# Expert down-projection pieces loaded with rows 2p and 2p+1 in partition p, and the activation transposed from every other column

## The chip, the core and the metric

The kernel runs on one core of one Trainium2 chip. The metric is device microseconds of that core, from the start of the program to its end. The kernel before takes 1797.82 us (median of 3 runs, 1796.47 to 1798.79).

## The reference

One encoder block over 512 tokens of width 1024: a norm, a wide input projection, a gated linear recurrence in both directions and a windowed attention, both merged and projected back, and then a mixture of 32 experts with the top 4 for each token. The change is in the experts:

```python
def expert_block(args):
    xblk, e = args
    hu = xblk @ w_up_gate[e] + b_up_gate[e]          # 1024 -> 2048
    g, u = hu[:, :D_FF_EXPERT], hu[:, D_FF_EXPERT:]
    g = jnp.minimum(g, SWIGLU_LIMIT)
    u = jnp.clip(u, -SWIGLU_LIMIT, SWIGLU_LIMIT)
    act = g * jax.nn.sigmoid(SWIGLU_ALPHA * g) * (u + 1.0)
    return act @ w_down[e] + b_down[e]               # 1024 -> 1024
```

`w_down[e]` is 1024 x 1024 in fp32, 4 MB; `w_up_gate[e]` is 1024 x 2048, 8 MB. The product `act @ w_down[e]` is a sum over 1024 rows of `w_down`, each with its own column of `act`. In which order and in which groups of 128 the rows are taken is free, as long as rows and columns go together.

## The kernel before

Each expert handles one block of up to 96 tokens (`BLK = 96`). All weights stream through SBUF once, in pieces of 1 MB: 128 partitions of 2048 fp32 values. An expert has 12 pieces, 8 of the up matrix (128 rows of 8 KB each, one row in a partition) and 4 of the down matrix (256 rows of 4 KB, two rows in a partition). A piece passes three stages. The SP queue loads it into one of 6 raw slots (`load_piece`, line 504, DMA at line 510), ACT copies it to fp32r as its high part `wH` (line 421), and DVE subtracts to get the low part `wL` (line 1687), each with 4 slots. SP waits before a load until DVE is done with the slot's former piece (`wait_split`, line 412). PE then multiplies three times for each pair of operands, high x high, high x low and low x high (`mm3`, lines 321 to 323).

The PE loop over experts (lines 1016 to 1020) does, for expert i: the up product of i, with the transposes of expert i-1's activation in it after its second piece (`a_part`, line 983), the transposes of the next expert's gathered tokens (`x_part`, line 936), and the down product of i-1 (`down_part`, line 995). The order of all engines is written out by hand.

`a_part` turns the activation `actv` (96 tokens x 1024) into eight tiles of 128 x 96. Each is one weight load of 96 x 128 from `actv` and one matmul with a 96 x 96 identity. Tile k becomes `aTH[:, k, :]` and `aTL[:, k, :]`. `down_part` multiplies tile `2 * q + kk` with half `kk` of piece q in its slot:

```python
def half_piece(kk, n):
    return slice(kk * D + n * 512, kk * D + (n + 1) * 512)
...
for kk in range(2):
    for n in range(2):
        last = mm3(bank[yb + n][0:BLK, :], high_[:, 2 * q + kk, :], low_[:, 2 * q + kk, :],
                   wH[:, slot, half_piece(kk, n)], wL[:, slot, half_piece(kk, n)], ...)
```

Of the kernel before, what the change touches and what calls it, by code (L numbers as in the profile page):

```python
# [35 lines left out]
P = 128  # L36
# [11 lines left out]
BLK = 96  # L48
# [55 lines left out]
def build(nc, x, norm_mix_gain, w_in, hg_lb_fwd, hg_lb_bwd, hg_norm_gain, attn_sink, w_out,  # L104
# [201 lines left out]
    bank = [nc_psum[:, i * 512:(i + 1) * 512] for i in range(8)]  # L306
# [7 lines left out]
    ident = cst[:, K_ID:K_TF]  # L314
# [94 lines left out]
    def first(i):  # L409
        return isinstance(i, int) and i == 0  # L410
# [52 lines left out]
    with nc.Block() as block:  # L463
# [3 lines left out]
        def _(sp):  # L467
# [45 lines left out]
                return w_up_gate[0][bass.ds(e, 1), p * P:(p + 1) * P, :].rearrange("o p n -> (o p) n")  # L513

            def down_src(e, q):
                return w_down[0][bass.ds(e, 1), q * 2 * P:(q + 1) * 2 * P, :].rearrange("o (k p) n -> p (o k) n", p=P)

            sp.wait_ge(w_lo, PRE_B + 8 * NH)
            for q in range(2):
# [28 lines left out]
            def load_body(e):  # L548
                for p in range(8):
                    load_piece(e, p, up_src(e, p))  # L550
                for q in range(4):
                    load_piece(e, 8 + q, down_src(e - 1, q))
# [12 lines left out]
            for q in range(4):  # L565
                load_piece(NE, q, down_src(NE - 1, q))
# [16 lines left out]
            def overflow(i, code):  # L583
                e = nc.s_assert_within(code >> NBC_BITS, 0, NE - 1, skip_runtime_bounds_check_because="codes are below NE * NBC")
                sp.wait_ge(x_ready, NT)
                for p in range(8):
                    load_piece(i, 4 + p, up_src(e, p))
                for q in range(4):
                    load_piece(i + 1, q, down_src(e, q))
# [12 lines left out]
        def _(pe):  # L602
# [5 lines left out]
            for k in range(KD):  # L608
                for j in range(NT):
                    if k == 0:  # L610
                        pe.wait_ge(xn0, j + 1)
                    last = nc.tensor.transpose(bank[k][:, j * P:(j + 1) * P], xt[:, j, k * P:(k + 1) * P], ident)
# [330 lines left out]
            def up_part(i, over=False, turn_last=False):  # L943
# [15 lines left out]
                for p in range(8):  # L959
                    if first(i):  # L960
                        pe.wait_ge(xTl_ready, p + 1)
                    wait_split(pe, k, b0 + p)
                    slot = (b0 + p) % SPLIT
                    for n in range(4):
                        cols = slice(n * 512, (n + 1) * 512)
                        last = mm3(bank[n][0:BLK, :], xTH[:, p, :], xTL[:, p, :], wH[:, slot, cols], wL[:, slot, cols], False, p == 7)
                    last.then_inc(p_used, 1)
                    if first(i) and p == 3:
                        table()
                    if turn_last and p == 1:  # L970
                        a_part(i - 1, 2 * i + KD)
                    if isinstance(i, int) and i == NE - 1 and p == 4:
                        turn_gates()
# [9 lines left out]
            def a_part(i, x_before):  # L983
                pe.wait_ge(act_ready, i + 1)
                pe.wait_ge(xTl_ready, x_before)
                if not first(i):
                    pe.wait_ge(aTl_ready, 2 * i)
                if isinstance(i, int) and i == NE - 1:
                    pe.wait_ge(gt_step, 3)
                for b_ in range(2):  # L990
                    for k in range(4 * b_, 4 * b_ + 4):
                        last = nc.tensor.transpose(bank[6 + b_][:, (k % 4) * BLK:(k % 4 + 1) * BLK], actv[0:BLK, k * P:(k + 1) * P], ident[0:BLK, 0:BLK])  # L992
                    last.then_inc(aT_done, 1)

            def down_part(i, over=False, turn_next=False, high_=aTH, low_=aTL):
                k, b0 = down_at(i, over)
                yb = Y_BANK[i] if isinstance(i, int) and i in LATE else 4
                if isinstance(i, int) and i == LATE[1]:
                    pe.wait_ge(sg_ready, NE)
                elif not first(i) and not over:  # L1000
                    pe.wait_ge(y_ready, i)
                pe.wait_ge(aTl_ready, 2 * i + 2)
                for q in range(4):
                    wait_split(pe, k, b0 + q)
                    slot = (b0 + q) % SPLIT
                    for kk in range(2):
                        for n in range(2):
                            last = mm3(bank[yb + n][0:BLK, :], high_[:, 2 * q + kk, :], low_[:, 2 * q + kk, :], wH[:, slot, half_piece(kk, n)],
                                       wL[:, slot, half_piece(kk, n)], 2 * q + kk == 0, 2 * q + kk == KD - 1)
                    last.then_inc(p_used, 1)  # L1010
                    if turn_next and q == 1:
                        a_part(i + 1, 2 * NE - 2 + KD)
# [58 lines left out]
            def overflow(i):  # L1071
                pe.wait_ge(aTl_ready, 2 * i)
                pe.wait_ge(x_ready, NT * (i - (NE - 1)))
                x_part(i)
                up_part(i, True)
                a_part(i, 2 * i + KD)
                down_part(i, True)
                pe.wait_ge(place_set, 4 * (i - LATE[0]) + (4 + TOPK))
                pe.wait_ge(yL_ready, i - LATE[0] + 1)
                for j in range(NT):  # L1080
                    combine(0, j, True, True)
# [1105 lines left out]
```

## Time and profile before

| | before |
|---|---|
| median of 3 runs | 1797.82 us |
| the profiled execution's own time | 1797.82 us |
| its span | 1796.1 us |
| PE busy | 1756.1 us (98%) |
| DVE busy | 1426.3 us (79%) |
| ACT busy | 1143.2 us (64%) |
| mean DMA rate over the span | 272 GB/s |
| one high part (ACT, line 421) / one low part (DVE, line 1687) | 1919 / 2288 ns |

Times are microseconds in one profiled execution, counted from the start of the span. PE is TensorE's matmul side and PEld its weight loads, which overlap with the matmuls. SPq is the queue of SyncE, which issues nearly all DMAs. A line number names the line of the kernel that made the instruction; where a helper makes it, as `mm3` does, the operands tell the use. In the chain of waits each piece is listed with the time for which nothing else held up the end, so eight transposes count there from the first start to the next instruction's start.

### The profile page before, as it was taken

How to read it: one execution, taken by the hardware profiler on the slowest of the kernel's cores; microseconds unless marked ns; L12 is line 12 of the kernel's file. 1: busy time of each engine (PE TensorE's matmuls, PEld its weight loads, DVE VectorE, ACT ScalarE, POOL GpSimd, SP SyncE). 2: the span in 40 equal slices, each digit the busy share in tenths (PEclk: the TensorE clock that was granted, in tenths of full speed). 3: DMA queues.
4: the chain of work that ended last, by engine and by line, in shares of the span. 5: the costliest groups of instructions: out<-in, count | busy, mean ns of one | idle time of the engine just before them, and what ended most of it. 6: DMA issues, size and time to landing. Idle time of an engine off the chain costs nothing.

```text
span 1796.1 us, 26530 instructions
## 1 busy us (share of the span) xinstructions
PE 1756.1 (98%) x8973; PEld 1286.9 (72%) x8973; DVE 1426.3 (79%) x1461; ACT 1143.2 (64%) x1122; POOL 316.3 (18%) x244
## 2 busy tenths in 40 slices
PE   6999999999999989999999999999999999999997
PEld 5777777777778856777777777777777777777765
DVE  4565665576557688988898889889888988898898
ACT  4534554454454556777777777777777777777783
POOL 0012102201210111211211121112111211211153
PEclk9999999999999989999999999999999999999999
DMA  7431332233116469999999999999999999999995
GB/s 207 130 87 55 105 93 73 67 105 104 36 61 224 178 244 342 402 382 380 365 368 367 379 365 369 370 365 380 359 376 371 366 369 378 366 370 367 376 341 235
DMA packets 159058, 488.44 MB, mean 272 GB/s; under 512 B 13186, under 2 KB 83122, under 8 KB 125520
## 3 DMA queue, kind: packets, MB, share of 16 engines
q1 hardware_dynamic: 151936, 471.48, 71.9%
q0 software_dynamic: 7088, 16.52, 2.7%
q8 instruction: 20, 0.33, 0.1%
q14 instruction: 14, 0.11, 0.0%
HBM read 479.43 MB, written 24.39 MB: 281 GB/s over the span
## 4 chain that ended last, share of the span: by engine, by line
PE 93%; DVE 3%; DMA 2%; issue 1%; SPq 1%; ACT 0%; POOL 0%; DVEq 0%; POOLq 0%; ACTq 0%
PE psum L321 27%; PE psum L323 26%; PE psum L322 26%; PE psum L956 1%; PE psum L690 1%; PE psum L720 1%; PE psum L706 1%; PE psum L940 1%; PE psum L992 1%; PE psum L673 1%; DVE wL L1687 1%; DMA wraw<-in_w_down 1%; PE psum L657 1%; PE psum L667 1%; PE psum L747 1%
## 5 line engine op out<-in xcount | busy, mean ns | idle before, releaser
L1687 DVE TENSOR_TENSOR wL<-wraw,wH 128x2048 fp32r<-128x2048 f32 x388 | 882.2, 2288 | 122.5 <-ACT wH L421 119.8
L421 ACT ACTIVATE wH<-wraw 128x2048 fp32r<-128x2048 f32 x388 | 743.9, 1919 | 296.2 <-PE psum L323 279.7
L321 PE MATMUL psum<-wH,xTH 128*96 128x512 f32 x1040 | 417.3, 401 | 2.9 <-DVE wL L1687 2.8
L323 PE MATMUL psum<-wH,xTL 128*96 128x512 f32 x1040 | 409.1, 393 | 0.0
L322 PE MATMUL psum<-wL,xTH 128*96 128x512 f32 x1040 | 408.9, 393 | 0.0
L321 PEld LDWEIGHTS psum<-wH,xTH 128*96 128x96 f32 x1040 | 168.4, 162 | 76.0 <-DVE wL L1687 2.8
L323 PEld LDWEIGHTS psum<-wH,xTL 128*96 128x96 f32 x1040 | 168.2, 162 | 72.7 <-issue 0.2
L322 PEld LDWEIGHTS psum<-wL,xTH 128*96 128x96 f32 x1040 | 168.4, 162 | 69.5
L321 PE MATMUL psum<-wH,aTH 128*96 128x512 f32 x496 | 197.1, 397 | 0.3 <-DVE wL L1687 0.3
L323 PE MATMUL psum<-wH,aTL 128*96 128x512 f32 x496 | 194.6, 392 | 0.0
L322 PE MATMUL psum<-wL,aTH 128*96 128x512 f32 x496 | 194.2, 391 | 0.0
L2095 POOL COPY ixg<-tab 128x2 int32 (+1 forms) x31 | 22.8, 734 | 557.6 <-PE psum L940 543.9
L321 PE MATMUL psum<-tsH,xnH 128*128 128x512 f32 (+1 forms) x288 | 112.2, 390 | 0.0
L321 PE MATMUL psum<-xnH,wsH 128*128 128x512 f32 x272 | 109.7, 403 | 0.1
L323 PE MATMUL psum<-tsH,xnL 128*128 128x512 f32 (+1 forms) x288 | 109.0, 379 | 0.0
L322 PE MATMUL psum<-tsL,xnH 128*128 128x512 f32 (+1 forms) x288 | 109.0, 378 | 0.0
L323 PE MATMUL psum<-xnH,wsL 128*128 128x512 f32 x272 | 106.2, 391 | 0.0
L322 PE MATMUL psum<-xnL,wsH 128*128 128x512 f32 x272 | 106.0, 390 | 0.0
L2099 POOL DMA_INDIRECT xg<-x2d,ixg x31 | 101.5, 3273 | 24.1 <-POOL ixg L2095 24.1
L323 PEld LDWEIGHTS psum<-wH,aTL 128*96 128x96 f32 x496 | 80.0, 161 | 35.0
L322 PEld LDWEIGHTS psum<-wL,aTH 128*96 128x96 f32 x496 | 80.2, 162 | 32.3
L321 PEld LDWEIGHTS psum<-wH,aTH 128*96 128x96 f32 x496 | 79.9, 161 | 32.7 <-DVE wL L1687 0.8
(272 smaller groups left out, 2178.3 us busy)
## 6 DMA issues: line engine op xcount, KB each, us to landing
wraw<-in_w_up_gate SPq DMA_DIRECT2D x256, 1024.0 KB, 6.9
wraw<-in_w_down SPq DMA_DIRECT2D x128, 1024.0 KB, 7.7
fraw<-in_w_in SPq DMA_DIRECT2D x68, 512.0 KB, 4.1
yd<-in_consts SPq DMA_DIRECT2D x8, 1024.0 KB, 8.4
wraw<-yd SPq DMA_DIRECT2D x3, 2048.0 KB, 11.0
wraw<-in_w_out SPq DMA_DIRECT2D x4, 1024.0 KB, 6.0
xt<-in_x SPq DMA_DIRECT2D x4, 512.0 KB, 6.5
hres<-in_x SPq DMA_DIRECT2D x4, 512.0 KB, 5.3
```

The costliest lines, as they stand in the source:

```text
L321: nc.tensor.matmul(ps, lh, rh, start=start, stop=False)
L322: nc.tensor.matmul(ps, lh, rl, start=False, stop=False)
L323: return nc.tensor.matmul(ps, ll, rh, start=False, stop=stop)
L421: nc.scalar.activation(wH[:, b % SPLIT, :], raw(b), ACT.Copy).then_inc(p_hi, 1)
L657: last = nc.tensor.matmul(bank[4 + 2 * d + c][:, j * P:(j + 1) * P], kt[rows_of, j, :], vv[rows_of, j, :], start=True, stop=True)
L667: nc.tensor.matmul(ps, ss[:, j, :], vv[:, j, :], start=True, stop=False, skip_group_check=True)
L673: last = nc.tensor.matmul(half, qd[:, tok], S[:, n, :], start=False, stop=True, skip_group_check=True)
L690: nc.tensor.matmul(bank[4 + a][:, 0:len(tiles) * P], aqT[half, n * P:(n + 1) * P], kcur[half, tiles[0] * P:(tiles[-1] + 1) * P], start=Tru ...
L706: last = nc.tensor.transpose(bank[2 + a][:, i * P:(i + 1) * P], sbuf_p[:, a, i * P:(i + 1) * P], ident)
L1687: V.tensor_tensor(wL[:, b % SPLIT, :], raw(b), wH[:, b % SPLIT, :].bitcast(F32), ALU.subtract).then_inc(p_lo, 1)
L2095: G.tensor_copy(ixg[:, :], src).then_inc(ix_ready, 1)
L2099: gp.indirect_dma_start(xg[0:BLK, :], None, x2d, bass.IndirectOffsetOnAxis(ap=ixg[0:BLK, 0:1], axis=0), bounds_check=last_token, oob_is_er ...
```

## The change

In the load of the down matrix (`down_src`), partition p of piece q held rows 256q + p and 256q + 128 + p, two runs of 4 KB. It now holds rows 256q + 2p and 256q + 2p + 1, which are neighbours in memory: one run of 8 KB, and the whole piece is one contiguous megabyte. Half kk of the slot thus holds the rows 256q + 2p + kk. The transposes follow: tile k, which was columns 128k to 128k + 127 of `actv`, is now the 128 columns 256 (k // 2) + k % 2 + 2p. Everything behind them is as it was.

```diff
             def down_src(e, q):
-                return w_down[0][bass.ds(e, 1), q * 2 * P:(q + 1) * 2 * P, :].rearrange("o (k p) n -> p (o k) n", p=P)
+                return w_down[0][bass.ds(e, 1), q * 2 * P:(q + 1) * 2 * P, :].rearrange("o (p k) n -> p (o k n)", k=2)
...
                     for k in range(4 * b_, 4 * b_ + 4):
-                        last = nc.tensor.transpose(bank[6 + b_][:, (k % 4) * BLK:(k % 4 + 1) * BLK], actv[0:BLK, k * P:(k + 1) * P], ident[0:BLK, 0:BLK])
+                        last = nc.tensor.transpose(bank[6 + b_][:, (k % 4) * BLK:(k % 4 + 1) * BLK], actv[0:BLK, (k // 2) * 2 * P + k % 2:(k // 2 + 1) * 2 * P:2], ident[0:BLK, 0:BLK])
```

No instruction is added, removed or moved on any engine. On SP the loads of the down matrix alone have another shape. This is expert 0's place, straight ahead of the loop over the other experts:

```order
 L540 DMA x2d<-xr 128x1024
 L510 DMA wraw<-in_w_up_gate 128x2048 x8
-L510 DMA wraw<-in_w_down 128x2x1024 x4
+L510 DMA wraw<-in_w_down 128x2048 x4
 L559 DMA over_list<-ovi 128x1
 L560 DMA gate_of<-gates 128x4x4
```

The four loads stand where they stood; what was 2 x 1024 values for each partition is one run of 2048, the shape of the up matrix's loads above them.

## Rows read from the trace of the kernel before

**Rows 1.** The page, part 1: busy time of each engine, share of the span.

```profile
PE 1756.1 (98%) x8973; PEld 1286.9 (72%) x8973; DVE 1426.3 (79%) x1461; ACT 1143.2 (64%) x1122; POOL 316.3 (18%) x244
```

**Rows 2.** Busy time by stretch; columns as the header row says.

```profile
core 0: us, PE busy (x) PEld busy (x) DVE busy (x) ACT busy (x) POOL busy (x), PEclk, DMA share, GB/s
657.94:693.30 35.36, 33.55 (x154) 22.90 (x152) 31.28 (x31) 20.89 (x15) 2.46 (x2) 1.00 0.89 257
693.40:1744.80 1051.40, 1051.40 (x4865) 741.93 (x4866) 933.79 (x564) 783.21 (x539) 201.28 (x125) 1.00 0.98 373
1744.80:1796.10 51.30, 39.38 (x160) 26.10 (x158) 44.89 (x37) 20.48 (x24) 20.47 (x8) 0.91 0.60 236
```

**Rows 3.** Chain of waits, one expert's period: start us, us, what.

```profile
1018.26 0.66 PE psum L992 x8
1035.54 0.66 PE psum L940 x8
...
1053.70 0.66 PE psum L992 x8
```

**Rows 4.** Waits, 700 to 1711 us: engine line waited for, us, times, longest.

```profile
ACT wH L421 <- PE psum L323: 253.1, 303, 0.9
...
ACT wH L421 <- DMA wraw<-in_w_up_gate: 4.2, 5, 1.7
ACT wH L421 <- DMA wraw<-in_w_down: 3.5, 4, 1.7
```

**Rows 5.** DMA issues of the page: count, KB each, us to landing.

```profile
wraw<-in_w_up_gate SPq DMA_DIRECT2D x256, 1024.0 KB, 6.9
wraw<-in_w_down SPq DMA_DIRECT2D x128, 1024.0 KB, 7.7
```

**Rows 6.** Waits of the SP queue, 700 to 1711 us.

```profile
SPq L510 <- DVE wL L1687: 803.6, 344, 3.7
```

**Rows 7.** Line 510's own issues on SP: ns min/median/max, first and last.

```profile
L510 SPq DMA_DIRECT2D wraw<-in_w_up_gate x256: 327/333/943, 565.3 to 1720.5; - x128
...
L510 SPq DMA_DIRECT2D wraw<-in_w_down x128: 367/376/384, 657.9 to 1744.9; - x128
```

**Rows 8.** Timeline of SP, first loads of the second matrix: start us, us.

```profile
657.94 12.50 SPq L510 DMA_DIRECT2D wraw<-in_w_down  x4
...
671.00 0.52 SPq L560 DMA_DIRECT2D gate_of<-gates  x1
```

**Rows 9.** Busy time by stretch around the first such loads.

```profile
676.00:679.00 3.00, 3.00 (x15) 2.10 (x14) 3.00 (x2) 2.16 (x2) 0.00 (x0) 1.00 2.25 106
679.00:682.00 3.00, 3.00 (x20) 2.28 (x19) 3.00 (x3) 0.05 (x1) 1.45 (x1) 1.00 0.05 22
```

**Rows 10.** Chain of waits, the last of expert 0's four such loads.

```profile
670.07 14.73 DMA wraw<-in_w_down
```

**Rows 11.** Timeline of ACT and PE: what stood still behind the late load.

```profile
684.82 1.91 ACT L421 ACTIVATE wH<-wraw 128x2048 fp32r<-128x2048 f32 x1 [5.77 <-DMA wraw<-in_w_down]
...
693.38 0.48 PE L321 MATMUL psum<-wH,xTH 128*96 128x512 f32 x1 [0.38 <-DVE wL L1687]
```

**Rows 12.** Waits of ACT on the pieces, 1711 to 1796 us.

```profile
ACT wH L421 <- PE psum L323: 10.1, 11, 2.3
...
DVE wL L1687 <- ACT wH L421: 4.1, 8, 1.3
```

**Rows 13.** Weight loads by line and shape: count, busy us, mean ns.

```profile
L322 PEld LDWEIGHTS psum<-wL,xTH 128*96 128x96 f32 x1040 | 168.4, 162 | 69.5
...
L322 PEld LDWEIGHTS psum<-tsL,xnH 128*128 128x128 f32 x288 | 54.3, 188 | 9.2
...
L992 PEld LDWEIGHTS psum<-cst,actv 96*128 96x128 f32 x256 | 24.8, 140 | 6.8 <-DVE actv L1896 1.9
...
L980 PEld LDWEIGHTS psum<-cst,gd 128*96 128x96 f32 x4 | 0.5, 126 | 0.2
```

**Rows 14.** Timeline of PE, one expert's eight transposes of the activation.

```profile
699.13 0.82 PE L992 MATMUL psum<-cst,actv 96*128 96x96 f32 x8
```

## Prediction

> **What bounds the kernel now.** I read the page's busy shares first, then busy time by stretch, then the chain of waits over one expert, and last what waits for DMA. TensorE is busy for 98% of the span [rows 1]. By stretch the picture is sharper [rows 2]: from 693.40 to 1744.80 us, which is the experts' loop, it is busy 1051.40 of 1051.40 us at a granted clock of 1.00. There is no idle time there to give back, whatever the transfers do. The chain over one expert consists of PE pieces alone, and the activation's eight transposes stand in it with 0.66 us at 1018.26, as the eight transposes of the gathered tokens do at 1035.54 [rows 3]. So the time of an expert is a sum of PE work, and the reader should look for two things only: whether the change alters PE work, and whether anything in the few stretches where PE idles hangs on the second matrix's loads.
>
> In the same window ACT, the first user of every piece, waited 3.5 us in 4 waits for the second matrix and 4.2 us in 5 waits for the first, of 1011 us; its 303 other waits were for PE to free a buffer [rows 4]. None of it reached PE.
>
> **The change, part by part.**
>
> *The loads.* 128 pieces of 1 MB each arrive in partition runs of 8 KB instead of two of 4 KB. Their shape is then that of the first matrix's pieces: same bytes, same 128 partitions, one run each. The page prices both: 7.7 us median to landing for the second matrix, 6.9 for the first [rows 5]. I take 6.9 for the new form, 0.8 less. The two medians are taken at different places of the queue, so 0.8 is an estimate; between 0 and twice that changes nothing below. In the loop a piece that lands 0.8 us sooner lies ready longer: the SP queue spent 803.6 us of 1011 waiting for DVE to free a slot [rows 6], so the loads run as fast as slots come free and not the reverse. Worth on the path: 0. What would be late next if that cover were gone: ACT's split, 7.7 us of waits in all [rows 4], and behind it DVE and PE.
>
> *Their issue.* One issue of such a load costs SP 376 ns, one of the first matrix's 333 [rows 7]; 4 x 43 ns an expert, in a queue that waits for most of the loop. Worth 0. The order and the waits of all five engines stay as they are.
>
> *The one place where a late load shows.* Expert 0's four loads of the second matrix are issued from 657.94 on, and a small write of gates follows them at 671.00 [rows 8]. Between 676 and 682 us the queues move 106 and then 22 GB/s [rows 9], and the last of the four lands 14.73 us after its release [rows 10]. ACT stands for 5.77 us before that piece, and 8.6 us later PE loses 0.38 us to DVE's low part [rows 11]. A faster load can give back that 0.38 us. The bound is all idle time of PE between the first such load and the steady loop, 35.36 - 33.55 = 1.81 us [rows 2]; the other bound is 0, since the hole at 676 to 682 us is no matter of run length (the first matrix's loads stand in it as well) and may lie as before or a little later. I take 0.3 us gained, near the 0.38 that the row shows. Before 657.94 no load of the second matrix exists, so that part can't change.
>
> *The end.* After 1744.80 PE idles 51.30 - 39.38 = 11.92 us [rows 2]. ACT's eleven waits for pieces there are all for PE, none for a DMA [rows 12]. Worth 0.
>
> *The transposes.* This is the only part on the path. Their number stays 8 x 32 = 256, with the activation as the weight load (96 x 128) and the identity streaming. What changes is that the load reads every other 4-byte column, 8 bytes apart, where it read neighbours. No row of before shows a weight load with such a step, so I bound it. How much room is there? Loads in transposes take 140 ns for 128 columns and 126 for 96 [rows 13]: (140 - 126) / 32 = 0.44 ns a column, so 56 ns of the 140 are reading, the rest a latency. Plain fp32 loads take 188 and 162: 0.81 ns a column, 104 ns for 128. Eight transposes take 0.82 us from the first start to the last end [rows 14] and 0.66 / 8 = 82.5 ns each on the chain [rows 3]. A read of 56 ns hides under 82.5 ns with 26 to spare.
> Lower bound: 0, a step can't make the read cheaper than neighbours, and the pace is not set by the load. Upper bound, if the step halves the rate: the read takes 104 (the plain fp32 rate) to 112 ns (twice 56), that is 22 to 30 ns over the pace, times 256 is 5.6 to 7.7 us, all of it exposed because PE has no idle time. Between these the room decides: the step may slow the read by up to 82.5 / 56 = 1.47 times at no cost. I take 0, since the rows give nothing that ties the rate to distance.
>
> The Trainium skill has a rule against this part: "SBUF — State Buffer", Door 1 (the note on cachelines), says that SBUF is read in lines of 16 bytes and that two accesses to a line are needed for the full rate, with a penalty where each access goes to a new line. No row here shows a stepped read, so the trace neither confirms nor denies it. With an 8-byte step two columns share a line, so by this rule the transposes stay free; by the same rule a step of 16 bytes would be the costly one. Its "DMA: Bandwidth & Descriptors", section Bandwidth (why small descriptors are slow), puts a fixed overhead on each descriptor; by it the loads gain a little from halving their number, and rows 5 agree in sign.
>
> **The sum.** The profiled execution took 1797.82 us, span 1796.1, which is also the median of the three runs (1796.47 to 1798.79). 1797.8 - 0.3 (start of the loop) + 0 (loads in the loop) + 0 (issue) + 0 (transposes) = 1797.5 us.
>
> **The rivals.**
> 1. *The transposes' weight load halves its rate* (slower). Place: line 992, each of the 256. It decides from 1.47 times the present read. For it: fp32 loads at 0.81 ns a column exist in this trace, so the path can run at that pace, and PE has no slack. Against it: the loads in transposes run at 0.44, and 26 ns are free. Time: 1797.5 + 5.6 to 7.7 = 1803.1 to 1805.2, middle 1804.
> 2. *Each stepped column costs a whole read of its own* (slower, rarer): four times the read, 224 - 82.5 = 141 ns, times 256 = 36 us, 1834. Only a step that defeats the read path entirely would do that; nothing in the rows speaks for it.
> 3. *The faster loads matter more than the rows say* (faster): expert 0's piece lands early, the loop starts 1.8 us sooner and nothing replaces it. Time: 1796.0. To get beyond 3.6 us something in a fully busy PE stretch would have to speed up with the shape of a transfer; matmuls of this loop would then have to start closer together. I see no row for it.
> 4. *The change doesn't do what it says*: the queue could cut a run of 8 KB into two pieces again, and the landing stays 7.7 us. The first matrix's 6.9 speaks against it. Time 1797.8, the same answer on the clock.
>
> **How the numbers follow.** What a measurement of this kernel can tell from no change is 0.2%, 3.6 us: 1794.2 to 1801.4. The forecast with rival 4 has 0.66, rival 3 within the bound 0.07, rival 3 beyond it (or an unknown gain) 0.05, rival 1 0.18, rival 2 with other unknown losses 0.04. So faster 0.05, same 0.73, slower 0.22. The range goes from 1795.0 (rival 3's 1796.0 less the runs' own 1 us) to 1804.5, which takes in most of rival 1.
>
> **What would show each step right or wrong.** The chain's entry for the eight transposes: 0.66 us if the step is free, 0.83 to 0.9 by rival 1; the mean of their weight load at 140 ns, or near 190. The transposes of the gathered tokens are the control: they must stay at 0.66. The period between two experts is 1053.70 - 1018.26 = 35.44 us [rows 3] if I am right, and 0.18 to 0.24 more by rival 1. The second matrix's landing should be about 6.9 us and its issue about 333 ns. ACT's 5.77 us wait should shrink and PE still be busy without a gap from about 693 to 1744 us. A PE idle total in the loop that is not zero, or matmuls of the loop at another pace, would make the forecast wrong in a way that none of the cases holds.

## The result and the profile after

The changed kernel takes 1805.93 us (median of 5 runs, 1804.88 to 1807.3) against 1796.47 us for the kernel before in its company (5 runs, 1795.38 to 1798.79). The ratio is 1.0049, 95% interval 1.0037 to 1.0061: 8.8 us slower (6.6 to 11). Forecast were 1797.5 us and no change, with 1804.5 as the upper end of the range. The profiled execution took 1806.29 us, its span is 1804.5.

First the chain of waits of the changed kernel over one expert (start us, us, what), which answers to [rows 3]:

```profile
697.87 0.92 PE psum L992 x8
715.41 0.66 PE psum L940 x8
...
733.58 0.92 PE psum L992 x8
```

The eight transposes of the activation (line 992) count 0.92 us where they counted 0.66. Those of the gathered tokens (line 940), which the change doesn't touch, still count 0.66. From one expert to the next it is 733.58 - 697.87 = 35.71 us, where it was 35.44. That is 0.27 us an expert and 32 x 0.27 = 8.6 us in all.

The weight loads of both kinds of transposes, by line and shape (count | busy us, mean ns | idle before), against [rows 13]:

```profile
L992 PEld LDWEIGHTS psum<-cst,actv 96*128 96x128 f32 x256 | 35.5, 211 | 5.2 <-DVE actv L1896 1.8
L940 PEld LDWEIGHTS psum<-cst,xg 96*128 96x128 f32 x248 | 24.4, 143 | 9.7 <-DMA xg<-x2d,ixg 4.8
```

211 ns in place of 140 for line 992; line 940 stays at the 143 ns it had before. And busy time by stretch (columns as in [rows 2]):

```profile
657.94:693.30 35.36, 34.70 (x159) 24.09 (x158) 32.02 (x30) 21.49 (x15) 2.49 (x2) 1.00 0.89 266
693.40:1744.80 1051.40, 1051.40 (x4832) 745.97 (x4831) 926.37 (x560) 777.13 (x534) 199.96 (x122) 1.00 0.97 370
```

PE is still busy without a gap in the loop, but in the same stretch it gets through fewer instructions: 4832 in place of 4865, and 33 matmuls of 0.23 us are 7.6 us. Nothing waits; PE itself has more to do.

The loads took the shape that the change asks for. The hardware queue's packets (count, MB, share of 16 engines) before, then after:

```profile
q1 hardware_dynamic: 151936, 471.48, 71.9%
q1 hardware_dynamic: 135552, 471.48, 71.3%
```

That is 16384 packets fewer for the same bytes, or 128 for each of the 128 pieces: one for each partition of a piece. A run of 8 KB is not cut in two again, and rival 4 of the prediction falls. The landing and the issues on SP:

```profile
wraw<-in_w_down SPq DMA_DIRECT2D x128, 1024.0 KB, 7.2
```

```profile
L510 SPq DMA_DIRECT2D wraw<-in_w_down x128: 327/333/339, 657.6 to 1751.7; - x128
```

The issue went from 376 to 333 ns [rows 7], and it does so in every run with 8 KB runs. The median landing went from 7.7 to 7.2 us [rows 5]. Over all profiled executions of this case it is 7.2 to 7.5 us in the five kernels with 8 KB runs and 7.3 to 8.0 us in the nine with 4 KB runs: lower by some 0.4 us, though the two spreads touch.

Behind expert 0's last load of the second matrix, ACT waited 4.85 us where it had waited 5.77 [rows 11], and PE's idle time between 657.94 and 693.3 us fell from 1.81 to 35.36 - 34.70 = 0.66 us. This can't be put down to the loads. In the kernels whose loads are those of before, that wait of ACT is anywhere from 2.75 to 5.77 us and the same idle time of PE from 0.83 to 1.81 us; in those with 8 KB runs it is 2.82 to 4.85 us and 0.66 to 2.19 us.

### The profile page after: what moved, and what is told of

Read it like the earlier page. It is cut to its first block, busy times and chain, and to the rows that moved or that the text cites. A ratio compares the mean times of both kernels' runs of the same rounds, so it can differ in the third digit from the quotient of the medians.

```text
span 1804.5 us, 26530 instructions
## 1 busy us (share of the span) xinstructions
PE 1766.1 (98%) x8973; PEld 1298.8 (72%) x8973; DVE 1426.2 (79%) x1461; ACT 1143.3 (63%) x1122; POOL 317.9 (18%) x244
## 4 chain that ended last, share of the span: by engine, by line
PE 95%; DVE 3%; DMA 1%; issue 1%; ACT 0%; SPq 0%; POOL 0%; DVEq 0%; POOLq 0%; ACTq 0%
PE psum L321 27%; PE psum L323 27%; PE psum L322 27%; PE psum L992 2%; PE psum L956 1%; PE psum L690 1%; PE psum L720 1%; PE psum L706 1%; PE psum L940 1%; PE psum L673 1%; DVE wL L1687 1%; PE psum L657 1%; PE psum L667 1%; DMA xg<-x2d,ixg 1%; PE psum L747 1%
```

## The experiments

Each kernel was run beside the kernel before on the same chip; a ratio is to that one, with its 95% interval. Short diffs are to the kernel before unless another is named.

### Loads alone

```diff
-  .rearrange("o (k p) n -> p (o k) n", p=P)
+  .rearrange("o (p k) n -> p (o k n)", k=2)
```

> The loads in 8 KB runs, the transposes as before (rows and columns no longer go together; the instructions and sizes are those of before). Theory A (all of the loss is in the stepped weight load of the transposes): the eight transposes count 0.66 us in the chain again, their weight load 140 ns, and the time is that of the kernel before, 0 to 1 us less (PE idled 1.15 us less between 657.94 and 693.3 us after the change). Theory B (the contiguous loads cost something, by the transfers' arrival or by contention): a part of the 9 us stays, and it would show as PE idle or matmuls further apart than 0.23 us.

1797.52 us against 1797.72, ratio 1.0002 (0.9993 to 1.0011). Its chain:

```profile
733.57 0.66 PE psum L992 x8
...
769.01 0.66 PE psum L992 x8
```

The period is 35.44 us again. The loads cost nothing and, within 0.1%, bring nothing. Theory B falls.

### Transposes alone

```diff
-  actv[0:BLK, k * P:(k + 1) * P]
+  actv[0:BLK, (k // 2) * 2 * P + k % 2:(k // 2 + 1) * 2 * P:2]
```

> The loads as before, the transposes from every other column (rows and columns no longer go together). Theory A: the whole loss, 8 to 9.5 us slower than before: 0.26 us in each of 32 groups of eight transposes, which count 0.92 us in the chain, with a weight load of about 211 ns. Theory B: less than 8 us, the rest belongs to the loads.

1804.6 us against 1797.72, ratio 1.0042 (1.0028 to 1.0056).

```profile
733.38 0.92 PE psum L992 x8
...
769.10 0.92 PE psum L992 x8
```

0.92 us and a period of 769.10 - 733.38 = 35.72 us: the loss of the changed kernel, from this line alone. Theory A holds. The loads of this kernel are those of before, and yet PE idles only 1.05 us between 657.94 and 693.3 us: the shorter idle time there comes without the 8 KB runs too.

### The cost doubled

```diff
 (against the changed kernel, line 940)
-  xg[0:BLK, k * P:(k + 1) * P]
+  xg[0:BLK, (k // 2) * 2 * P + k % 2:(k // 2 + 1) * 2 * P:2]
```

> The changed kernel, with the transposes of the gathered tokens stepping by two as well, which leaves their rows unmatched to the weights. The suspected cost is doubled: theory A says another 31 groups of eight at 0.26 us, 8 us more than the changed kernel, 16 to 18 us over the kernel before, the period of an expert at 35.98 us. If the loss is bound to the activation's place (its writer, its buffer), it is less.

1814.42 us against 1796.66, ratio 1.0096 (1.0081 to 1.0112): 17 us over the kernel before, twice the loss. The period of an expert is 35.97 us.

```profile
L992 PEld LDWEIGHTS psum<-cst,actv 96*128 96x128 f32 x256 | 35.5, 211 | 5.0 <-DVE actv L1896 1.9
L940 PEld LDWEIGHTS psum<-cst,xg 96*128 96x128 f32 x248 | 34.6, 212 | 8.4 <-DMA xg<-x2d,ixg 5.2
```

The tokens' loads now take 212 ns like the activation's. The buffer and its writer have no part in it (the tokens are written by a DMA, the activation by DVE).

### How the cost depends on the step

```diff
-  actv[0:BLK, k * P:(k + 1) * P]
+  actv[0:BLK, (k // 4) * 4 * P + k % 4:(k // 4 + 1) * 4 * P:4]   (4 apart)
+  actv[0:BLK, k:8 * P:8]                                         (8 apart)
+  actv[0:BLK, k * 126 + 1:k * 126 + 129]                         (neighbours, odd start)
```

> The loads as before; each transpose reads its 128 columns 4 apart (16 bytes), which leaves the order of rows and columns unmatched. Theory P (neighbouring fp32 columns are fetched in pairs, any step above 1 loses that): same as step 2, weight load 211 ns, eight transposes 0.92 us, 8 to 9.5 us slower than before. Theory L (the fetch is limited by the 16-byte lines it touches: a quarter line a column at step 1, half at step 2, one at step 4): from step 2 the read of about 132 ns doubles to 264, the weight load takes about 345 ns, a group of eight transposes about 2 us, and the kernel is some 42 us slower than before.

> The loads as before, the transposes' columns 8 apart (32 bytes); rows and columns unmatched. By the pair theory the same as steps 2 and 4: weight load about 214 ns, eight transposes 0.92 us. If distance counts at all, it is more here.

> The loads as before, the transposes read 128 neighbouring columns that begin at an odd column (126k + 1), so that no pair of columns is aligned to 8 bytes as before; the activation is not covered whole. If fp32 columns are fetched in aligned pairs of 8 bytes, this costs next to nothing (65 fetches in place of 64): 140 ns, 0.66 us. If the fast read needs an aligned start, it shows as the step does: 211 ns, 0.92 us.

The weight loads of line 992 with the columns 4 apart, 8 apart, and side by side from an odd start:

```profile
L992 PEld LDWEIGHTS psum<-cst,actv 96*128 96x128 f32 x256 | 35.7, 214 | 5.0 <-DVE actv L1896 1.9
```

```profile
L992 PEld LDWEIGHTS psum<-cst,actv 96*128 96x128 f32 x256 | 33.3, 203 | 5.4 <-DVE actv L1896 1.9
```

```profile
L992 PEld LDWEIGHTS psum<-cst,actv 96*128 96x128 f32 x256 | 24.9, 139 | 6.8 <-DVE actv L1896 1.9
```

214 ns at a step of 4, 203 at 8, against 211 at 2. The kernel with step 4 takes 1805.09 us against 1797.72, ratio 1.0040 (1.0025 to 1.0056); the other two are single runs (1802.77 and 1794.86 us, against 1796.66). The chain at step 8:

```profile
733.51 0.86 PE psum L992 x8
...
769.16 0.86 PE psum L992 x8
```

A greater distance costs next to nothing more (3 ns at step 4): theory L, with 345 ns and 42 us, is refuted. The load of neighbours from an odd column takes 139 ns. So what is lost is adjacency, and it is lost with the first step; alignment to 8 bytes isn't needed. One thing was not expected: at step 8 the group counts 0.86 us and not 0.92, and the period is 35.65 us, 0.21 over the kernel before and not 0.27. Every period of that trace shows it, and no run says why. That the fast read takes two neighbouring values at a time fits the rest, but it doesn't explain this, and the runs show rates, not the fetch itself.

### By the column or by the load?

Half the activation is left out here: seven of eight transposes take 64 columns. The first diff is side by side, the second with a step of two.

```diff
-  bank[6 + b_][:, ...], actv[0:BLK, k * P:(k + 1) * P]
+  bank[6 + b_][0:64 if k else P, ...], actv[0:BLK, k * P:k * P + (64 if k else P)]
+  bank[6 + b_][0:64 if k else P, ...], actv[0:BLK, k * P:k * P + (128 if k else 2 * P):2]
```

> The loads as before; seven of the eight transposes of a group take 64 neighbouring columns in place of 128, the first takes 128 (half of the activation is left out). The read at 0.44 ns a column: 112 ns for a weight load of 64 columns, 28 less than for 128. The pace of transposes stays at 82 ns, since the streaming identity sets it.

> The same with a step of two. If the step costs by the column, as two single reads in place of one pair (0.88 to 1.03 ns a column against 0.44), a weight load of 64 columns takes 140 to 150 ns and the read of 56 to 66 ns hides under the 82 ns of the identity: eight transposes count 0.66 to 0.7 us and the loss is gone. If the step costs a fixed time for each weight load, the load takes 112 + 74 = 186 ns and the group stays near 0.92 us.

Side by side, then with the step:

```profile
L992 PEld LDWEIGHTS psum<-cst,actv 96*64 96x64 f32 x224 | 19.4, 111 | 2.7
...
L992 PEld LDWEIGHTS psum<-cst,actv 96*128 96x128 f32 x32 | 4.5, 141 | 4.0 <-DVE actv L1896 1.9
```

```profile
L992 PEld LDWEIGHTS psum<-cst,actv 96*64 96x64 f32 x224 | 20.3, 138 | 1.0
...
L992 PEld LDWEIGHTS psum<-cst,actv 96*128 96x128 f32 x32 | 6.4, 200 | 4.0 <-DVE actv L1896 1.9
```

Side by side it is 111 ns for 64 columns and 141 for 128: (141 - 111) / 64 = 0.47 ns a column. With the step it is 138 for 64 and 200 for 128: (200 - 138) / 64 = 0.97 ns a column. With the shortest load of the changed kernel, 194 ns, it is (194 - 138) / 64 = 0.88. So a column takes about twice the time of before, 112 to 124 ns for 128 columns, and 64 stepped columns (138 ns) take what 128 neighbours take (140 ns). Both kernels were run once, 1798.91 us side by side and 1797.74 with the step, against 1796.36; the loss is read from the chain, here with 64 stepped columns:

```profile
734.32 0.66 PE psum L992 x8
...
769.77 0.66 PE psum L992 x8
```

0.66 us and a period of 35.45: a stepped read of 64 columns, 56 to 62 ns, hides under the 82.5 ns of the streaming identity, and the loss is gone. The cost goes by the column, and only what stands out over the matmul is paid.

### The step hidden under matmuls

```diff
 (against the changed kernel, in the third piece of the up product; the eight in a row after the second piece go)
+  for n in range(4):
+      matmul(bank[n], xTH, wH)
+      turn_one(2 * n)
+      matmul(bank[n], xTH, wL)
+      turn_one(2 * n + 1)
+      matmul(bank[n], xTL, wH)
```

> The changed kernel, with the eight transposes of the loop no longer back to back: each stands between two matmuls of the up product's third piece (same operands, same results, two of every three gaps taken). Theory A (the stepped weight load costs only where it is longer than what runs in front of it): the read of the transpose now lies under a matmul of 230 ns, each transpose adds 82 to 90 ns again, the period of an expert goes from 35.71 us back to 35.44 to 35.5, and the kernel is within 0.2% of the one before. Theory D (the stepped load holds the array or the fetch for itself and is not hidden): each transpose still adds 115 ns, period 35.71, 8 to 9.5 us slower than before. The transposed activation is complete some 2 us later, which ACT and DVE could turn into a wait of PE at line 956 or 1002; neither theory expects it, as they stand idle for 4 us or more an expert.

> Control for the spread transposes: the same placement between matmuls, but loads and transposes as in the kernel before (two runs of 4 KB, neighbouring columns). If the 0.09 us an expert that the spread kernel kept over the one before (period 35.53 us against 35.44) come from the change of neighbours between transposes and matmuls, they stay here: period 35.53 us, about 3 us over the kernel before. If they are what the hidden step still costs, the period is 35.44 and the time that of before.

With the step: 1799.98 us against 1796.66, ratio 1.0019 (1.0010 to 1.0028). The control with neighbouring columns: 1798.84 against 1797.35, ratio 1.0008 (0.9999 to 1.0017). The chain of the stepped one, where the transposes are line 994:

```profile
768.16 0.09 PE psum L994
768.25 0.24 PE psum L973
768.49 0.09 PE psum L994
768.57 0.23 PE psum L975
```

Each transpose adds 0.08 to 0.09 us and not 0.115, though its load is still slow:

```profile
L994 PEld LDWEIGHTS psum<-cst,actv 96*128 96x128 f32 x256 | 50.3, 199 | 10.8 <-DVE actv L1912 1.9
```

The period between two groups of line 940:

```profile
749.77 0.66 PE psum L940 x8
...
785.29 0.66 PE psum L940 x8
```

```profile
750.94 0.66 PE psum L940 x8
...
786.44 0.66 PE psum L940 x8
```

35.52 us with the step (35.53 in most periods of its chain), 35.50 without it, 35.44 in the kernel before. Some 0.06 us an expert are the price of the mixed order, 0.02 to 0.03 what the step still costs. Theory D falls: a slow weight load in front of which 230 ns of matmul run is nearly free.

### The step moved to DVE

```diff
 (loads as in the changed kernel; the transposes are those of the kernel before)
-  V.scalar_tensor_tensor(out=actv[0:BLK, :], in0=sg[0:BLK, :], scalar=S_LIMIT, in1=ucl[0:BLK, :], ...
+  V.scalar_tensor_tensor(out=actv[0:BLK, :].rearrange("b (k m) -> b k m", k=2),
+                         in0=sg[0:BLK, :].rearrange("b (m k) -> b k m", k=2), scalar=S_LIMIT,
+                         in1=ucl[0:BLK, :].rearrange("b (m k) -> b k m", k=2), ...
...
-  high_[:, 2 * q + kk, :], low_[:, 2 * q + kk, :]
+  high_[:, 4 * kk + q, :], low_[:, 4 * kk + q, :]
```

> The loads in 8 KB runs as in the changed kernel, but the step moves from PE's weight load to DVE: the instruction that makes the activation reads its two inputs at even columns first, then at odd ones, and writes them side by side, so PE's transposes read neighbours. Theory A: as before or up to 1 us less, transposes at 0.66 us; DVE's instruction of 1.22 us stays within 0.2 us, or up to doubles, which DVE's idle time in the loop (about 4 us an expert) covers. Rival C (a step of two costs DVE as it costs PE, and the activation is late for PE): DVE's instruction takes 2.3 us, PE shows idle before the transposes, up to 1 us an expert, 32 us in all.

1797.07 us against 1797.72, ratio 1.0000 (0.9991 to 1.0009). DVE's instruction in this kernel (ns min/median/max, first and last):

```profile
L1896 DVE SCALAR_TENSOR_TENSOR actv<-sg,ucl x32: 1214/1215/1222, 652.1 to 1749.6; 96x1024 f32<-96x1024 f32 x32
```

In the kernel with the loads alone, where it reads side by side, the median is 1215 ns too. DVE reads both inputs two apart for nothing; rival C falls. This is the way to have the 8 KB runs without a step on PE: by the two ratios (1.0000 and 1.0049) 8.8 us faster than the changed kernel. It doesn't beat the kernel before, since the loads have nothing to bring there.

### The step in the weight loads of the matmuls

```diff
-  mm3(bank[yb + n][0:BLK, :], high_[:, 2 * q + kk, :], low_[:, 2 * q + kk, :], ...
+  mm3(bank[yb + n][0:BLK, :], every_other(high_, q, kk), every_other(low_, q, kk), ...
+  every_other(t, q, kk): t[:, 2 * q:2 * q + 2, :].rearrange("p a s -> p (a s)")[:, kk:2 * BLK:2]
```

> The kernel before, with the step put into the 48 weight loads of each expert's down product in place of the transposes: each fp32r load of 96 columns takes every other column of the two tiles it lies in (rows unmatched). These loads take 162 ns side by side. If plain fp32 loads lose to a step what the transposes' loads lost (the rate halves, 0.81 to 1.6 ns a column), they take about 240 ns; the read of 156 ns still lies under 230 ns of matmul, so the time stays as before. If plain loads fetch single columns already, a step costs them nothing: 162 ns. In both cases the transposes stay at 140 ns and 0.66 us.

A single run, 1795.28 us against 1797.35. First the up product's loads (xTH), without the step, then the down product's (aTH), where the step is:

```profile
L322 PEld LDWEIGHTS psum<-wL,xTH 128*96 128x96 f32 x1040 | 168.6, 162 | 69.4
...
L322 PEld LDWEIGHTS psum<-wL,aTH 128*96 128x96 f32 x496 | 82.2, 166 | 30.3
```

166 ns with the step; without it the down product's loads took 162 too in the kernel before. That is 4 ns where the transposes' loads lost 71. The load that runs at 0.81 ns a column side by side has almost nothing to lose; the one at 0.44 comes down to about that rate. The two kinds differ in more than rate: the first belongs to a matmul with fp32r operands, the second to a transpose with fp32 ones. No run separates these, so what makes the second kind fast stays open.

## Why the prediction was wrong

**What bounds the kernel** was read rightly: PE has no idle time in the loop, and each ns that it works longer is paid in full. The loss shows just there.

**The loads, in the loop: 0.** Right: ratio 1.0002 for the loads alone. The landing came down by about half of the 0.8 us reckoned, which changes nothing. **Their issue: 0**, right, with 333 ns as said. Rival 4 is out by the packet count, rival 3 by the ratio of the loads alone.

**The start of the loop: 0.3 us gained.** No run shows this term. ACT's wait and PE's idle time shrank in the profile of the changed kernel, as the prediction had named as a sign, but they vary as much between kernels that keep the 4 KB runs (ACT 2.75 to 5.77 us, PE 0.83 to 1.81 us). The 5.77 us from which the term was read are the longest wait of all; that it shrank was luck. On the clock the loads alone show no gain.

**The transposes: 0.** This is the step that failed. The prediction bounded it rightly from both sides, 0 and 5.6 to 7.7 us, and then took the lower end with "the rows give nothing that ties the rate to distance". The rows did hold a hint that was used only to price the rival: two rates of weight loads, 0.44 and 0.81 ns a column for the same 4-byte values. The faster one needs a reason, and adjacency is the one that a step takes away. The runs show it: a step of two brings the fast load to 0.88 to 0.97 ns a column, and the slow kind barely feels one (166 against 162 ns). (The prediction calls the slow kind plain fp32; in the kernel its operands are fp32r.)

**The rival's size** was a little low. It reckoned with 22 to 30 ns a transpose over the pace. Eight count 0.92 us, so one takes 115 and 115 - 82.5 = 32.5 ns are exposed; times 256 that is 8.3 us. The profile's period gives 8.6, the ratio 8.8. The rival's upper price was 2.5 ns a transpose short, and the range had been ended at 1804.5, short of the rival's own 1805.2; the measured 1805.93 lies past both. Of its signs, the group came out at 0.92 us where 0.83 to 0.9 were named. The mean load came out at 211 ns where near 190 was named; where a stepped load has room in front of it, between matmuls, the mean is 199.

**The rule of the Trainium skill** ("SBUF — State Buffer", Door 1, the note on cachelines) was weighed and followed. By its two accesses to a line of 16 bytes, a step of 8 bytes is free and one of 16 is where the penalty begins. The measurements decide against it here: 211 ns at 8 bytes, 214 at 16, 203 at 32, all against 140. For the matmuls' loads (166 against 162 at 8 bytes) and for DVE's reads (1215 ns either way) a step of 8 bytes is free or nearly so, as it says.

## What to carry to other kernels

Where an engine is busy without a gap, an access pattern on it is a change of its work, even if no instruction is added; price it before the transfers that it is meant to help, which may be hidden anyway. A load that runs at twice the rate of its like may do so on a condition, as it did here: keep the stationary operand of fp32 transposes side by side, and put a needed step where there is slack, in the engine that writes the operand or in the order of loads under long matmuls. And check that the transfer which the change improves is waited for at all: here ACT waited 3.5 us of 1011 for it. Where a term rests on one wait in one execution, compare that wait over several executions of kernels that share the code: here it moved by 3 us with nothing changed in the loads.

## What the runs showed of the hardware

- The weight load of an fp32 transpose takes 140 ns for 128 neighbouring columns (0.44 to 0.47 ns for each column more) and, back to back, 211, 214 and 203 ns for columns 2, 4 or 8 apart (0.88 to 0.97 ns a column at 2). An odd start doesn't matter (139 ns).
- The weight load of an fp32r matmul, 96 columns, takes 162 ns side by side and 166 with a step of two.
- Only the part of a weight load that stands out over what PE streams in front of it is paid: stepped, it adds 32.5 ns where a transpose of 82.5 ns runs in front of it, and some 3 ns (0.02 to 0.03 us over eight) where a matmul of 230 ns does.
- A load of 1 MB in 128 runs of 8 KB costs the SP queue 333 ns, in 256 runs of 4 KB 376 ns; the median landing is 7.2 to 7.5 us in five kernels with the former and 7.3 to 8.0 us in nine with the latter.
